# Attention in two blocks: a round's value products and scores stand together behind its transposes

## The chip, the cores and the metric

The kernel runs on one core of a Trainium2 chip. The metric is the device time of one execution in microseconds (us). The engines are TensorE (PE, matmuls and transposes), VectorE (DVE), ScalarE (ACT), GpSimd (POOL) and SyncE (SP, which issues most DMAs).

## The reference

Two transformer blocks on 512 tokens of width 1024, in float32. The two places that matter here are their attentions. The first block has a local attention (8 heads) and a dilated attention (12 heads in 3 groups). The second block has two layers; its first is an attention with 16 query heads over 512 latent and 256 context tokens:

```
def neighbourhood_attention(q, k, v, rpb):
    ...
    scores = jnp.einsum('brqhd,brkhd->bhrqk', qg, kn).astype(f32) * (dh ** -0.5) + bias[None]
    scores = jnp.where(mask, scores, NEG_INF)
    p = jax.nn.softmax(scores, axis=-1).astype(v.dtype)
    o = jnp.einsum('bhrqk,brkhd->brqhd', p, vn)

def gqa_attend(q, k, v):
    s = jnp.einsum('bkgqd,bksd->bkgqs', q, k, preferred_element_type=jnp.float32) * (HEAD_DIM_2 ** -0.5)
    p = jax.nn.softmax(s, axis=-1).astype(v.dtype)
    return jnp.einsum('bkgqs,bksd->bkgqd', p, v)

def dilated_window_attention(q, k, v, window, dilation):
    ...
    p = jnp.exp(scores - lse[..., None]).astype(v.dtype)
    o = jnp.einsum('nhbqk,nbkhd->nbqhd', p, vb).reshape(-1, lp, h, dh)[:, :seg]
```

The dilated attention runs once for each group, and the groups' outputs are weighted by their softmax denominators. Around the attentions stand dense projections, gated feed-forward layers and, at the end, a gated recurrent layer (the HGRN mixer), which the change doesn't touch.

## The kernel before

The program is made in two steps. A planner (`build_program`) writes a list of steps, each with the semaphores that it waits for. Then every engine gets its own instructions of each step, in the order of that list. So one list sets the order on all queues: if a step stands ahead of another in the list, its parts stand ahead on PE, on DVE and on ACT.

Dense products are exact to float32 by a split: an operand is a rounded part and a rest (`SHI` and `SLO` of a weight, `hh` and `hl` of an activation, `HLh` and `HLl` of the input), and a product is three matmuls (lines 2517 to 2519), with 512 or 256 columns. ACT rounds a weight tile (line 2084) and POOL makes the rest (line 2254).

Attention works on pairs of heads (two items, h = 0 and 1). A pair passes through four steps:

- `s1`, a `Score` step: PE multiplies queries and keys (line 2537, from partitions 0 to 63 for one head and 64 to 127 for the other), into two areas of PSUM (`scores`, banks 0 to 3). DVE takes the maximum (line 2368; in the first block with the mask added, line 2365), ACT takes the exponential into `e` and its sum into `m` (line 2119).
- `s2`, one to three `Flip` steps: PE transposes `e` (line 2544), four blocks of 128 columns at a time into one bank (three in the dilated attention), and ACT and DVE in turn copy the bank into `pt` (lines 2125 and 2373).
- `shares`, two `Share` steps: DVE takes the reciprocal of the sum (line 2377), ACT makes the diagonal matrix `dg` from it (line 2129).
- `s3`, a `Pv` step, and `normed`, an `OutNorm` step: PE multiplies `dg` by ones (line 2550) and the values by `pt` (line 2554), both with 64 output partitions a head; ACT and DVE normalise into `o` (lines 2133 and 2381), and that frees the bank. `finish` then writes an `OutSplit` step: ACT rounds `o` into `hh` (line 2137), POOL makes the rest.

Round i of the loop in `attention` has the transposes of pair i - 2, the value products of pair i - 3 and the scores of pair i. There are 72 rounds with scores: 16 of the local attention (256 or 384 keys), 8 of the dilated one (768 keys) and 48 of the second block's. There, six pairs belong to one query tile, with 768, 256, 768, 768, 256 and 768 keys.

`attention` is a generator. At each `yield` the function `weave` may place dense work: it keeps a count of work for both sequences and goes on with the one that is behind. In the second block the dense sequence is, for each query tile, the projection of the next one with its head norm and rotary step (`qk2`: a square on ACT at line 2107, a matmul at line 2525, a logarithm and an exponential on ACT at lines 2111 and 2113, a multiplication on DVE at line 2352, a matmul at line 2529) and the output projection of the one before (`out2`, whose sums DVE adds at line 2395).

Transposes, value products, head norms and dense sums share four PSUM banks (4 to 7). `take` hands them out in the order in which `give` put them back, so a change of order in the plan also changes which step waits for which bank. The first PE instruction that writes a bank waits for whoever read it last.

Of the kernel before, what the change touches and what calls it, by code (L numbers as in the profile page):

```python
# [241 lines left out]
def build_program(nc, t_in, out):  # L242
# [3 lines left out]
    def put(step):  # L246

        plan.append(type(step)(*map(frozen, step)))

    def tick(name, n=1):  # L250

        count[name] = count.get(name, 0) + n
        last[name[0]] = (name, count[name])
        return (name, count[name])

    def all_now():
        return [last[e] for e in "pavg" if e in last]
# [13 lines left out]
    def place(name, shape, dt, at):  # L271
        return nc.alloc_sbuf_tensor_at(name, shape, dt, offset=at)

    def fixed(name, n, dt=F32, size=4):
        at = base[0]
        base[0] += (n * size + 31) // 32 * 32
        return place(name, [128, n], dt, at), at

    XL, _ = fixed("XL", 8 * NT)
    XC, XC_at = fixed("XC", 8 * NC)  # L280
    HLh, _ = fixed("HLh", 8 * NT, F32R)
    HLl, _ = fixed("HLl", 8 * NT, F32R)
# [6 lines left out]
    CONST, _ = fixed("CONST", 640)  # L289
    COL, _ = fixed("COL", NCOLS)  # L290
    MOD1, _ = fixed("MOD1", 48)
    MOD2, _ = fixed("MOD2", 96)
    MOD3, _ = fixed("MOD3", 96)
    COEF, _ = fixed("COEF", 48)
    SMALL, _ = fixed("SMALL", 16)
    ROPE, _ = fixed("ROPE", 1024)
    LBS, _ = fixed("LBS", 40)
# [10 lines left out]
    def take():  # L308
        return banks[free_banks.pop(0)]

    def give(b, *tok):
        b.free = list(flat(tok))
        free_banks.append(banks.index(b))
# [91 lines left out]
    def arena(specs, free, end=END):  # L405
        at, rings = AR, {}
        for name, (n, cols, dt, size) in specs.items():
            aps = []
            for i in range(n):
                aps.append(place(f"{name}_{names[0]}", [128, cols], dt, at)[:, :])  # L410
                names[0] += 1
                at += (cols * size + 31) // 32 * 32
            rings[name] = Ring(aps, free)
        assert at <= end, at - end
        return rings

    names = [0]
    emitted = set()

    def after(key):  # L420
        while key not in emitted:
            yield "wait"
# [61 lines left out]
    def slots(cells):  # L484
        for i, c in enumerate(cells):
            c.raw, c.at = f"d_ada{names[0]}", 0
            names[0] += 1
        return cells
# [240 lines left out]
    def attention(items, W, finish):  # L729
        st, exps, dgs = {}, {}, {}  # L730

        def s1(pair):
            mms, t_q, used = [], [], []
            for it in pair:
                mm, t = it["scores"]()
                work[0] += 2 * sum(at.stop - at.start for at, _, _ in mm)
                mms.append(mm)
                t_q += t
                used.append((it["e"](), W["m"].next(), scores.next()))
            n = pair[0]["n"]  # L740
            masks, t_mask = zip(*(it.get("mask", (None, None)) for it in pair))
            t_mm, t_max, t_exp = tick("p_score", 2), tick("v_max", 2), tick("a_exp", 2)
            put(Score(mms, [ps.ap[:, 0:n] for _, _, ps in used], [e.ap[:, 0:n] for e, _, _ in used],
                      [m.ap for _, m, _ in used], masks, t_q, [ps.free for _, _, ps in used], t_mm,
                      [e.free for e, _, _ in used], [m.free for _, m, _ in used], t_mask, t_max, t_exp))
            for h, (it, (e, m, ps)) in enumerate(zip(pair, used)):
                one = lambda t: (t[0], t[1] - 1 + h)
                ps.free = [one(t_max) if masks[h] else one(t_exp)]
                if "masked" in it:
                    it["masked"](one(t_max))  # L750
                st[id(it)] = (e, one(t_exp))
                exps[id(it)] = (m, one(t_exp))
                it["scored_by"](t_mm)
# [31 lines left out]
        def shares(it):  # L785

            m, t_exp = exps.pop(id(it))
            d = W["dg"].next()
            t_rec, t = tick("v_rec"), tick("a_share")
            put(Share(m.ap, d.ap, t_exp, t_rec, d.free, t))  # L790
            m.free = [t]
            d.rdy = [t]
            dgs[id(it)] = d

        def s3(pair):

            ps, at, toks = zip(*(st.pop(id(it)) for it in pair))
            ds = [dgs.pop(id(it)) for it in pair]
            nk = pair[0]["n"] // 128  # L800
            b = take()
            vals = [[it["values"](j) for j in range(nk)] for it in pair]
            work[0] += 512 * nk + 512
            t_mm = tick("p_pv")
            put(Pv([p.ap[:, 128 * a:128 * (a + nk)] for p, a in zip(ps, at)], nk, b.ap, [[v for v, _ in vs] for vs in vals], [d.ap for d in ds], list(toks),
                   vals[0][0][1], [d.rdy for d in ds], b.free, t_mm))
            for c in (*ps, *ds):
                c.free = [t_mm]
            return b, t_mm

        def normed(b, t_mm):
            o = W["o"].next()
            t_rb, t = tick("a_rb"), tick("v_onorm")
            put(OutNorm(b.ap, o.ap, t_mm, o.free, t_rb, t))
            give(b, t)
            return o, t

        pairs = [items[i:i + 2] for i in range(0, len(items), 2)]
        n = len(pairs)
        for i in range(n + 4):  # L820
            turn, read = 0 <= i - 2 < n, 0 <= i - 3 < n
            turns = s2(pairs[i - 2]) if turn else iter(())
            for _ in turns:
                yield
                break
            if read:
                done = normed(*s3(pairs[i - 3]))
                yield
            yield from turns
            if turn:  # L830
                for it in pairs[i - 2]:
                    shares(it)
            if read:
                finish(pairs[i - 3][0], *done)
                if "done" in pairs[i - 3][1]:
                    emitted.add(pairs[i - 3][1]["done"])
            if i < n:
                for key in pairs[i][0].get("needs", ()):
                    yield from after(key)
                s1(pairs[i])  # L840
                if "scored" in pairs[i][1]:
                    emitted.add(pairs[i][1]["scored"])
                yield

    def out_split(o, t_o, src, hi, lo, t_free):
        t1, t2 = tick("a_ohi"), tick("g_olo")
# [144 lines left out]
    def marked(items, needs, name):  # L991
# [31 lines left out]
    W = arena({"va": (1, 4 * 512, F32, 4), "qa": (4, 512, F32, 4), "vb": (1, 3 * 4 * 256, F32, 4),  # L1023
               "qb": (6, 512, F32, 4), "mk": (1, 1536, F32, 4), "bi": (5, 384, F32, 4), "e": (4, 384, F32, 4),
               "f": (4, 512, F32, 4), "pt": (3, 768, F32, 4), "r": (2, 512, F32, 4), "o": (2, 128, F32, 4), "dg": (2, 128, F32, 4),
               "m": (8, 8, F32, 4)}, [])
# [11 lines left out]
    early = slots([Cell(place(f"early{i}", [128, USZ], F32, AR + 4 * USZ * i)[:, :]) for i in range(12)])  # L1038
# [422 lines left out]
    W = arena({"hh": (6, 512, F32R, 4), "hl": (6, 512, F32R, 4), "f": (4, 512, F32, 4), "r": (2, 512, F32, 4)}, blk, c_at)  # L1461
# [43 lines left out]
    for c in W["r"].cells:  # L1505
# [14 lines left out]
    W = arena({"f": (4, 512, F32, 4), "r": (2, 512, F32, 4), "hh": (2, TT, F32R, 4), "hl": (2, TT, F32R, 4),  # L1520
               "q": (2, TT, F32, 4), "k": (2, TT, F32, 4), "v": (1, 6 * 256, F32, 4), "e": (4, TT, F32, 4),
               "pt": (2, 2 * TT, F32, 4), "o": (2, 128, F32, 4), "dg": (2, 128, F32, 4), "m": (8, 8, F32, 4)}, blk, c_at)
# [128 lines left out]
    W = arena({"hh": (6, TT, F32R, 4), "hl": (6, TT, F32R, 4), "f": (4, TT, F32, 4), "r": (2, 512, F32, 4)}, all_now(), c_at)  # L1651
    hid = hids(W)

    def with_mask(main):
        for i, _ in enumerate(main):
            if i == 20:
# [12 lines left out]
    W = arena({"v": (1, 6 * 256, F32, 4), "xy": (4, 2 * TT, F32, 4), "kk": (2, TT, F32, 4), "q": (2, NT, F32, 4),  # L1669
               "sg": (2, NT, F32, 4), "t": (2, TT + 1, F32, 4), "ek": (1, TT + 1, F32, 4), "eq": (1, NT, F32, 4),  # L1670
               "R": (1, 2 * NT, F32, 4), "A": (1, NT, F32, 4), "kt": (1, TT + 1, F32, 4), "S": (4, 128, F32, 4),
               "f": (1, NT, F32, 4), "r": (1, NT, F32, 4), "hh": (2, NT, F32R, 4), "hl": (2, NT, F32R, 4),
               "pe": (4, 8, F32, 4), "de": (4, 8, F32, 4)}, blk)
# [347 lines left out]
    W = arena({"hh": (6, NT, F32R, 4), "hl": (6, NT, F32R, 4), "f": (4, NT, F32, 4), "r": (2, 512, F32, 4)}, all_now())  # L2021
# [678 lines left out]
```

## Time and profile before

| What | Value |
|---|---|
| median of 3 runs | 2769.22 us (2765.15 to 2774.45) |
| span of the profiled execution | 2768.6 us |
| PE busy | 2622.1 us, 95% of the span |
| DVE, ACT, POOL busy | 56%, 40%, 36% |
| mean granted TensorE clock | 0.983 |

The profiled execution's span lies 0.6 us under the median of the runs, so the two can be set against each other without a correction. A granted clock of 1.00 is 2.4 GHz, of 0.50 it is 1.2 GHz. Busy shares of PE are high everywhere because matmuls overlap each other; what a stage loses is seen in the gaps between its instructions.

### The profile page before, as it was taken

What the parts mean: (1) busy time and instruction counts of PE and PEld (TensorE: products, weight loads), DVE (VectorE), ACT (ScalarE), POOL (GpSimd) and SP (SyncE); (2) the same over time, 40 slices, a digit from 0 to 9 for tenths busy, and PEclk for the clock granted to TensorE, in tenths of its full rate; (3) what the DMA queues carried; (4) which work ended last, traced back from release to release, by engine and by line L of the source; (5) the groups of instructions that cost most, each with busy time, mean ns of one, the idle gap of its engine ahead of it and who ended that gap; (6) DMA issues with size and microseconds to landing.
All of it is one profiled execution on the core that took longest, in us unless ns stands there. A gap on an engine that the chain in (4) does not pass through costs nothing. (4 is left out here: it accounts for less than half of the span.)

```text
span 2768.6 us, 39433 instructions
## 1 busy us (share of the span) xinstructions
PE 2622.1 (95%) x15278; PEld 2194.3 (79%) x15278; DVE 1545.5 (56%) x2406; ACT 1108.5 (40%) x2041; POOL 988.8 (36%) x571
## 2 busy tenths in 40 slices
PE   7997989899999999997999999998899997899998
PEld 5765778888888867776988888898788886788887
DVE  5454256654565355656765555656768677622324
ACT  4553442422323455555312112235555556522222
POOL 4344634445545312223323323342212212444444
PEclk9998999999999999999999999999999999999999
DMA  8633224343333100001333333311111110122222
GB/s 303 222 138 130 73 96 159 122 145 130 130 136 116 39 16 24 24 32 44 115 126 118 123 114 122 129 69 62 39 46 62 54 54 32 61 99 95 95 99 76
DMA packets 81465, 267.83 MB, mean 97 GB/s; under 512 B 8704, under 2 KB 16512, under 8 KB 81280
## 3 DMA queue, kind: packets, MB, share of 16 engines
q1 hardware_dynamic: 78944, 259.68, 26.8%
q10 hardware_dynamic: 2048, 4.33, 0.4%
q8 instruction: 122, 2.00, 0.3%
q0 software_dynamic: 288, 1.31, 0.1%
q14 instruction: 63, 0.52, 0.1%
HBM read 260.57 MB, written 4.72 MB: 96 GB/s over the span
## 5 line engine op out<-in xcount | busy, mean ns | idle before, releaser
L2254 POOL TENSOR_TENSOR SLO<-RAW,SHI 128x1024 fp32r<-128x1024 f32 (+1 forms) x290 | 704.9, 2433 | 1078.4 <-ACT SHI L2084 1073.0
L2084 ACT ACTIVATE SHI<-RAW 128x1024 fp32r<-128x1024 f32 (+1 forms) x334 | 344.9, 1037 | 969.6 <-PE PS L2519 967.9
L2517 PE MATMUL PS<-HLh,SHI 128*128 128x512 f32 (+1 forms) x1800 | 704.3, 391 | 11.5 <-POOL SLO L2254 5.6
L2519 PE MATMUL PS<-HLh,SLO 128*128 128x512 f32 (+1 forms) x1800 | 680.8, 378 | 0.0
L2518 PE MATMUL PS<-HLl,SHI 128*128 128x512 f32 (+1 forms) x1800 | 680.8, 378 | 0.0
L2517 PEld LDWEIGHTS PS<-HLh,SHI 128*128 128x128 f32 x1800 | 342.5, 190 | 82.6 <-issue 15.5
L2519 PEld LDWEIGHTS PS<-HLh,SLO 128*128 128x128 f32 x1800 | 341.8, 190 | 63.8
L2518 PEld LDWEIGHTS PS<-HLl,SHI 128*128 128x128 f32 x1800 | 342.7, 190 | 60.7 <-issue 5.8
L2517 PE MATMUL PS<-hh,SHI 128*128 128x512 f32 (+1 forms) x1024 | 366.2, 358 | 8.2 <-POOL SLO L2254 3.9
L2519 PE MATMUL PS<-hh,SLO 128*128 128x512 f32 (+1 forms) x1024 | 357.2, 349 | 0.0
L2518 PE MATMUL PS<-hl,SHI 128*128 128x512 f32 (+1 forms) x1024 | 355.3, 347 | 0.0
L2395 DVE SCALAR_TENSOR_TENSOR XL<-PS,MOD,XL 128x512 f32<-128x512 f32 (+1 forms) x320 | 209.8, 667 | 194.8 <-PE PS L2519 194.1
L2402 DVE TENSOR_TENSOR hl<-f,hh 128x512 fp32r<-128x512 f32 x88 | 163.9, 1863 | 121.6 <-ACT hh L2153 121.6
L2517 PEld LDWEIGHTS PS<-hh,SHI 128*128 128x128 f32 x1024 | 192.9, 188 | 43.0 <-issue 10.2
L2400 DVE TENSOR_TENSOR f<-f,PS 128x512 f32<-128x512 f32 x88 | 54.3, 617 | 306.8 <-PE PS L2519 285.0
L2518 PEld LDWEIGHTS PS<-hl,SHI 128*128 128x128 f32 x1024 | 193.0, 189 | 27.4 <-issue 1.2
L2519 PEld LDWEIGHTS PS<-hh,SLO 128*128 128x128 f32 x1024 | 192.8, 188 | 26.7
L2517 PE MATMUL PS<-HCh,SHI 128*128 128x256 f32 x560 | 165.1, 295 | 11.3 <-DVE XL L2395 7.8
L2333 DVE CUSTOM_DVE_ANT_0 ADA<-cb,ADA,COL 128x1024 f32<-128x1024 f32 x96 | 175.2, 1825 | 0.0
L2519 PE MATMUL PS<-HCh,SLO 128*128 128x256 f32 x560 | 160.2, 286 | 0.0
L2518 PE MATMUL PS<-HCl,SHI 128*128 128x256 f32 x560 | 160.2, 286 | 0.0
L2333 DVE CUSTOM_DVE_ANT_0 cdump<-cb,ADA,COL 128x1024 f32<-128x1024 f32 x96 | 141.3, 1472 | 13.9 <-DMA ADA<-in_k_w 13.9
(261 smaller groups left out, 3944.9 us busy)
## 6 DMA issues: line engine op xcount, KB each, us to landing
RAW<-in_k_w SPq DMA_DIRECT2D x318, 512.0 KB, 3.5
ADA<-in_k_w SPq DMA_DIRECT2D x132, 512.0 KB, 4.3
early<-in_k_w SPq DMA_DIRECT2D x12, 512.0 KB, 15.1
RAW<-in_k_w SPq DMA_DIRECT2D x16, 256.0 KB, 2.6
XL<-in_xT SPq DMA_DIRECT2D x4, 512.0 KB, 8.1
bi<-in_k_bias SPq DMA_DIRECT2D x16, 128.0 KB, 4.4
out<-XL SPq DMA_DIRECT2D x16, 128.0 KB, 1.8
bi<-in_k_bias SPq DMA_DIRECT2D x8, 192.0 KB, 4.2
```

Of the source, the lines that this page charges most:

```text
L2084: eng.activation(u.hi, u.w, ACT.Copy).then_inc(S["a_hi"], 1)
L2254: eng.tensor_tensor(u.lo, u.w, u.hi.bitcast(F32), ALU.subtract).then_inc(S["g_lo"], 1)
L2333: eng.tensor_tensor_reduce(w if j == n - 1 else st.dump, c, w, 1.0, st.bias, ALU.mult, ALU.add, st.mod[:, j:j + 1]).then_inc(S["v_ada"], 1)
L2395: eng.scalar_tensor_tensor(out=st.x, in0=st.src, scalar=st.gate, in1=st.x, op0=ALU.mult, op1=ALU.add).then_inc(S["v_res"], 1)
L2400: eng.tensor_tensor(st.f, st.f, st.src, ALU.mult).then_inc(S["v_up"], 1)
L2402: eng.tensor_tensor(st.lo, st.f, st.hi.bitcast(F32), ALU.subtract).then_inc(S["v_ulo"], 1)
L2517: eng.matmul(st.out, lh, rh, start=st.first and j == 0, stop=False)
L2518: eng.matmul(st.out, lh, rl, start=False, stop=False)
L2519: i = eng.matmul(st.out, ll, rh, start=False, stop=st.last and j == n - 1)
```

## The change

The loop of `attention` is written anew. A round first writes all its transposes (with a chance for dense work behind each group of them), then the value products of pair i - 3, and at once behind them the scores of pair i; only then `shares` and `finish`, and one `yield`. Before, the value products stood behind the first group of transposes, with dense work after them, and the scores were the last step of the round, behind `shares` and `finish`.

Two cases (`early`) keep the value products behind the first group of transposes: where the ring `pt` is too narrow for both heads of a pair (`held`; the dilated attention), and where the queries or keys that the scores need aren't in the plan yet (`needs`).

```
@@ -820,13 +820,24 @@
         for i in range(n + 4):
             turn, read = 0 <= i - 2 < n, 0 <= i - 3 < n
             turns = s2(pairs[i - 2]) if turn else iter(())
-            for _ in turns:
-                yield
-                break
-            if read:
+            needs = pairs[i][0].get("needs", ()) if i < n else ()
+            held = W["pt"].peek().ap.shape[1] < 2 * pairs[min(i, n + 1) - 2][0]["n"]
+            early = read and (held or any(key not in emitted for key in needs))
+            if early:
+                for _ in turns:
+                    yield
+                    break
                 done = normed(*s3(pairs[i - 3]))
                 yield
             yield from turns
+            for key in needs:
+                yield from after(key)
+            if read and not early:
+                done = normed(*s3(pairs[i - 3]))
+            if i < n:
+                s1(pairs[i])
+                if "scored" in pairs[i][1]:
+                    emitted.add(pairs[i][1]["scored"])
             if turn:
                 for it in pairs[i - 2]:
                     shares(it)
@@ -834,13 +845,7 @@
                 finish(pairs[i - 3][0], *done)
                 if "done" in pairs[i - 3][1]:
                     emitted.add(pairs[i - 3][1]["done"])
-            if i < n:
-                for key in pairs[i][0].get("needs", ()):
-                    yield from after(key)
-                s1(pairs[i])
-                if "scored" in pairs[i][1]:
-                    emitted.add(pairs[i][1]["scored"])
-                yield
+            yield
```

No engine gets an instruction more or less; lines below the diff have numbers higher by 5. Three places show the new order.

**Place 1.** PE's queue in the middle of the second block's attention, around the scores (L2537) of one pair with 768 keys. L2550 and L2554 are value products, L2525 is the head norm's matmul, L2529 the rotary one, L2517 to L2519 are dense. This stands there before:

```order
L2550 MATMUL PS<-dg_192,CONST 64x128 [waits s_v_flip,s_a_share]
L2550 MATMUL PS<-dg_193,CONST 64x128
L2554 MATMUL PS<-pt_188,v_183 64x128 x12
L2525 MATMUL PS<-f_169,CONST 128x256 [waits s_a_hln,s_a_hsq]
L2537 MATMUL PS<-k_181,q_179 128x512 [waits s_a_exp]
L2537 MATMUL PS<-k_181,q_179 128x512
L2537 MATMUL PS<-k_181,q_179 128x256 x2
L2529 MATMUL PS<-f_170,CONST 128x512 [waits s_v_head]
L2517 MATMUL PS<-hh_176,SHI_60 128x512 [waits s_a_ohi,s_g_olo,s_v_onorm,s_g_lo]
L2518 MATMUL PS<-hl_178,SHI_60 128x512
L2519 MATMUL PS<-hh_176,SLO_63 128x512
L2517 MATMUL PS<-hh_176,SHI_60 128x256 [waits s_a_hln]
```

And this stands there now:

```order
L2555 MATMUL PS<-dg_192,CONST 64x128 [waits s_v_flip,s_a_share]
L2555 MATMUL PS<-dg_193,CONST 64x128
L2559 MATMUL PS<-pt_188,v_183 64x128 x12
L2542 MATMUL PS<-k_181,q_179 128x512 [waits s_a_exp]
L2542 MATMUL PS<-k_181,q_179 128x512
L2542 MATMUL PS<-k_181,q_179 128x256 x2
L2530 MATMUL PS<-f_169,CONST 128x256 [waits s_a_hln,s_a_hsq]
L2534 MATMUL PS<-f_170,CONST 128x512 [waits s_v_head]
L2522 MATMUL PS<-hh_176,SHI_60 128x512 [waits s_a_ohi,s_g_olo,s_v_onorm,s_g_lo]
L2523 MATMUL PS<-hl_178,SHI_60 128x512
L2524 MATMUL PS<-hh_176,SLO_63 128x512
L2522 MATMUL PS<-hh_176,SHI_60 128x256 [waits s_a_hln]
```

The scores follow the value products directly, and the head norm of the 256 context columns, whose bank the last row waits for (`s_a_hln`), moved behind the scores.

**Place 2.** ACT's queue at the same point. The two rows that write `e` are the exponentials of those scores. Before:

```order
L2111 ACTIVATE r_174<-PS,SMALL 128x512
L2113 ACTIVATE r_174<-r_174 128x512
L2133 ACTIVATE o_190<-PS 128x128
L2111 ACTIVATE r_173<-PS,SMALL 128x256
L2113 ACTIVATE r_173<-r_173 128x256
L2129 ACTIVATE dg_192<-CONST,m_196 128x128
L2129 ACTIVATE dg_193<-CONST,m_197 128x128
L2137 ACTIVATE hh_175<-o_190 128x128
L2119 ACTIVATE e_186,m_200<-PS,m_200 128x768
L2119 ACTIVATE e_187,m_201<-PS,m_201 128x768
L2125 ACTIVATE pt_188<-PS 128x512
```

Now:

```order
L2116 ACTIVATE r_174<-PS,SMALL 128x512
L2118 ACTIVATE r_174<-r_174 128x512
L2138 ACTIVATE o_190<-PS 128x128
L2124 ACTIVATE e_186,m_200<-PS,m_200 128x768
L2124 ACTIVATE e_187,m_201<-PS,m_201 128x768
L2134 ACTIVATE dg_192<-CONST,m_196 128x128
L2134 ACTIVATE dg_193<-CONST,m_197 128x128
L2142 ACTIVATE hh_175<-o_190 128x128
L2116 ACTIVATE r_173<-PS,SMALL 128x256
L2118 ACTIVATE r_173<-r_173 128x256
L2130 ACTIVATE pt_188<-PS 128x512 x2
```

Both exponentials moved ahead of `dg`, of the rounding of `o`, and of the logarithm and exponential of the head norm (`r_173`).

**Place 3.** PE's queue near the end of this attention, where no dense work is left: from the transposes of one round to its scores. Before:

```order
L2544 MATMUL PS<-CONST,e_184 128x128 [waits s_v_flip]
L2544 MATMUL PS<-CONST,e_184 128x128 x3
L2550 MATMUL PS<-dg_192,CONST 64x128 [waits s_v_onorm,s_a_share]
L2550 MATMUL PS<-dg_193,CONST 64x128
L2554 MATMUL PS<-pt_189,v_183 64x128 [waits s_a_flip,s_v_flip]
L2554 MATMUL PS<-pt_189,v_183 64x128 x11
L2544 MATMUL PS<-CONST,e_184 128x128 x2
L2544 MATMUL PS<-CONST,e_185 128x128 x6
L2537 MATMUL PS<-k_182,q_180 128x512 [waits s_a_exp]
```

Now:

```order
L2549 MATMUL PS<-CONST,e_184 128x128 [waits s_v_flip]
L2549 MATMUL PS<-CONST,e_184 128x128 x3
L2549 MATMUL PS<-CONST,e_184 128x128 [waits s_a_flip]
L2549 MATMUL PS<-CONST,e_184 128x128
L2549 MATMUL PS<-CONST,e_185 128x128 x2
L2549 MATMUL PS<-CONST,e_185 128x128 [waits s_v_flip]
L2549 MATMUL PS<-CONST,e_185 128x128 x3
L2555 MATMUL PS<-dg_192,CONST 64x128 [waits s_v_onorm,s_a_share]
L2555 MATMUL PS<-dg_193,CONST 64x128
L2559 MATMUL PS<-pt_189,v_183 64x128 x12
L2542 MATMUL PS<-k_182,q_180 128x512 [waits s_a_exp]
```

The value products moved from behind the first four transposes to behind all twelve, and nothing stands between them and the scores.

## Rows read from the trace of the kernel before

**Rows 1.** The head of the page.
```profile
span 2768.6 us, 39433 instructions
```

**Rows 2.** Busy time by stretch (PE first): the second attention, one tile's six rounds.
```profile
950.00:1290.00 340.00, 318.19 (x2519) 236.61 (x2517) 191.62 (x414) 193.13 (x501) 77.63 (x85) 0.99 0.08 26
1093.90:1138.10 44.20, 43.22 (x336) 32.42 (x335) 26.30 (x56) 24.93 (x64) 10.16 (x11) 1.00 0.08 25
```

**Rows 3.** PE's timeline, second block: start us, duration us, count, [idle before].
```profile
1092.35 1.56 PE L2537 MATMUL PS<-k,q 64*128 64x512 f32 x8
1093.84 0.39 PE L2517 MATMUL PS<-HCh,SHI 128*128 128x256 f32 x1
1094.06 0.28 PE L2518 MATMUL PS<-HCl,SHI 128*128 128x256 f32 x1
1094.18 0.28 PE L2519 MATMUL PS<-HCh,SLO 128*128 128x256 f32 x1
...
1094.66 0.60 PE L2544 MATMUL PS<-CONST,e 128*128 128x128 f32 x4
1095.09 1.02 PE L2525 MATMUL PS<-f,CONST 128*128 128x512 f32 x2
1096.50 0.44 PE L2550 MATMUL PS<-dg,CONST 128*64 128x128 f32 x4 [0.39 <-DVE pt L2373]
...
1098.75 0.67 PE L2525 MATMUL PS<-f,CONST 128*128 128x256 f32 x2 [0.49 <-ACT r L2111]
1099.35 1.56 PE L2537 MATMUL PS<-k,q 64*128 64x512 f32 x8
```

**Rows 4.** ACT's timeline in the same stretch, and behind scores of 256 keys.
```profile
1092.82 0.30 ACT L2137 ACTIVATE hh<-o 128x128 fp32r<-128x128 f32 x1
...
1096.61 0.20 ACT L2119 ACTIVATION_READ_ACCUMULATOR e<-PS,m 128x1 f32 x1
1096.70 1.05 ACT L2084 ACTIVATE SHI<-RAW 128x1024 fp32r<-128x1024 f32 x1
...
1097.91 0.69 ACT L2111 ACTIVATE r<-PS,SMALL 128x512 f32<-128x512 f32 x1
1098.63 0.63 ACT L2113 ACTIVATE r<-r 128x512 f32<-128x512 f32 x1
...
1099.45 0.47 ACT L2111 ACTIVATE r<-PS,SMALL 128x256 f32<-128x256 f32 x1
...
1101.00 0.69 ACT L2129 ACTIVATE dg<-CONST,m 128x128 f32<-128x128 f32 x2 [0.62 <-DVE m L2377]
...
1108.76 0.19 ACT L2119 ACTIVATION_READ_ACCUMULATOR e<-PS,m 128x1 f32 x1
```

**Rows 5.** DVE's timeline in the same stretch.
```profile
1099.30 0.75 DVE L2352 SCALAR_TENSOR_TENSOR f<-PS,SMALL,r 128x512 f32<-128x512 f32 x1 [2.94 <-ACT r L2113]
...
1100.41 0.48 DVE L2352 SCALAR_TENSOR_TENSOR q<-PS,SMALL,r 128x256 f32<-128x256 f32 x1 [0.16 <-ACT r L2113]
```

**Rows 6.** PE's timeline: scores of 256 keys in the second block.
```profile
1106.43 0.70 PE L2537 MATMUL PS<-k,q 64*128 64x256 f32 x4
```

**Rows 7.** PE's timeline: dilated attention.
```profile
350.02 1.57 PE L2537 MATMUL PS<-qb,qb 64*128 64x512 f32 x12
...
352.00 0.44 PE L2550 MATMUL PS<-dg,CONST 128*64 128x128 f32 x4
```

**Rows 8.** PE's timeline: the second block's attention where dense work has ended, first and last.
```profile
1253.82 1.03 PE L2537 MATMUL PS<-k,q 64*128 64x512 f32 x6
...
1286.73 1.48 PE L2554 MATMUL PS<-pt,v 128*64 128x128 f32 x24
```

**Rows 9.** The longest total wait on PE, 950 to 1290 us.
```profile
PE PS L2550 <- ACT dg L2129: 7.0, 6, 1.9
```

**Rows 10.** PE's longest single wait there; and PE's busy time, then the granted clock.
```profile
1006.05 0.70 PE L2550 MATMUL PS<-dg,CONST 128*64 128x128 f32 x4 [2.65 <-ACT r L2111]
...
1006.00:1009.40 3.40, 3.35 (x29) 0.50 0.22 63
```

## The prediction

> **What bounds the kernel now.** I read the head of the page first: the span is 2768.6 us [rows 1], 0.6 us under the median of the runs, 2769.22, so I add to the median. Then the busy time by stretch. The change touches two stretches, the attentions of the first block and that of the second. In the 340.00 us of the second PE is busy 318.19 us, DVE and ACT less than 195 each [rows 2]. In the middle of the second, one query tile's six rounds take 44.20 us with 43.22 of PE [rows 2]. So PE sets the time, its work doesn't change, and the change can only win or lose what PE waits.
>
> The timeline of such a stretch shows how little it waits: 0.39 us before the value products (for a copy of transposes) and 0.49 us before the head norm of the context columns (for ACT's logarithm) [rows 3]; the same two come back in each query tile. The list of waits names `dg` as what PE waited for longest in the second block, 7.0 us in 6 waits [rows 9].
>
> **Gain: fewer changes of the array's shape.** Scores use half the rows of the array, value products half the columns, all else the whole. The first dense matmul behind scores of 256 columns is followed by the next after 0.22 us (1093.84 to 1094.06), the later ones after 0.12 us (1094.06 to 1094.18) [rows 3], so a way back costs about 0.1 us. I take the same for a way in, which no row here shows clean. I counted neighbours in PE's whole order: pairs of different shape go from 284 to 236, and value products directly ahead of scores from 4 to 50. Two excursions become one with a change inside it. If that inner change costs 0.1 us, the sum is 48 x 0.1 = 4.8 us; if it costs nothing, 98 x 0.1 = 9.8 us less (284 to 186). I take 4.8.
>
 The exit of 0.1 us agrees; no row here shows the inner change.
>
> **Loss 1: `dg` behind the exponentials.** `shares` now stands behind `s1`, so on ACT the `dg` of pair i - 2 waits for the exponentials of pair i (place 2), and the next round's value products need it. With 768 keys the scores end at 1093.91, the last exponential at 1096.81, 2.90 us later; two `dg` take 0.69 [rows 3, 4]. So the value products can't start until 3.65 us behind the scores' end. With 256 keys it is 1107.13 to 1108.95 and the same 0.69, about 2.55 us [rows 4, 6]. Where more PE work than that stands between, it costs nothing. Where not:
>
> - No dense work left, end of the second attention. Before, it takes from 1254.85 to 1288.21, 33.4 us [rows 8]. Value products take 1.7 us with 768 keys (0.27 for `dg`, 1.48 after it) and I put 0.8 with 256; scores 1.56 and 0.70 [rows 3, 6, 8]. Now the round is a chain: 3.65 + 0.8 + 0.7, then 2.55 + 1.7 + 1.6, 3.65 + 1.7 + 1.6, 3.65 + 0.8 + 0.7, 2.55 + 1.7 + 1.6, 3.65 + 1.7, and at the end about 4.5 for twelve transposes and two more value products: 38.6 us. +5 us.
> - The same at its start, three or four rounds: +3 us.
> - The dilated attention. `held` is true, so its value products stay behind the first transposes, but `shares` moved all the same. In its last rounds scores end at 351.59 and value products start at 352.00, 0.41 us later [rows 7]; now not before 3.7 us. Six of eight rounds start them earlier than that (0.97, 0.52, 1.85, 1.85, 0.41, 0.41 us), 16 us short together. Some waits for copies inside these rounds fall away, about 4 us. +12 us.
> - One round in each query tile has two context chunks and four transposes between scores and value products, 2.65 us of work: 1 us short, five times. +5 us.
>
> **Loss 2: banks released late.** This is the largest term. In each of six query tiles the head norm of 256 columns moved behind the scores (place 1), and its logarithm on ACT behind their exponentials and `dg` (place 2). The second dense chunk behind it takes the bank that this logarithm frees. Walked from the end of the scores before, t = 0:
>
> - PE: 18 dense matmuls of 256 columns 2.1 us, four transposes 0.43, head norm 0.86 [rows 3], so 3.45; value products wait for `dg` until 3.65, end 5.35; scores until 6.95.
> - ACT: exponentials 2.90, `dg` 3.6, `hh` 3.9, weight rounding and square 5.1, logarithm 5.8, exponential 6.4 [rows 4]. DVE multiplies until 7.1, normalises until 7.3 [rows 5], and only then takes the maxima. So the last exponential of the new scores ends at 7.3 + 2.85 = 10.15, `dg` 10.85, `hh` 11.1, the logarithm of the 256 columns (0.47 [rows 4]) 11.55.
> - PE is through head norm, rotary matmul and first chunk at 9.2 and waits for that bank until 11.55: 2.35 us. The next transposes wait 0.55 for a bank that DVE's multiplication frees (exponential 0.42, then 0.48 [rows 5]), and 0.15 and 0.25 for two more.
>
> With the 0.2 above that is 3.5 us; it replaces the 0.39 and 0.49 of before [rows 3], so 2.6 net, six times: +16 us. After scores of 256 keys twelve transposes stand together and the dense chunk behind them needs the bank of the first four. Its copy is on ACT behind exponentials, `dg`, `hh` and a square: 3.9 us behind the scores, where PE is there after 2.8. 1.1 us, five times: +5 us.
>
> **Local attention.** Mostly 3.3 us of work stand between scores and value products, enough for its shorter exponentials. Two head norms come earlier than their square. I put +3 us, between 0 and 6.
>
> **Sum.** -4.8 + 5 + 3 + 12 + 5 + 16 + 5 + 3 = +44 us. 2769 + 44 = 2813 us. What hid these latencies before is the half round of transposes, value products and dense work between the `dg` and its use; that cover is what moved.
>
> **The rivals.**
>
> *A. Faster.* If PE isn't held by `dg` and banks, because waits of a few tenths sit in slack that my walks don't see, the shape changes decide: -4.8, and the 0.88 us in each of six tiles goes too, -5.3: 2759 us. Against it: where no dense work is left there is nothing to overlap with. It decides if value products there start less than 1 us behind the scores. 7%.
>
> *B. Only `dg` is late.* The bank waits of loss 2 vanish because PE, held at one place, isn't held again at the next: -4.8 - 5.3 + 25 + 3 = +18, 2787 us. For it: I walked one tile, from an even start. 20%.
>
> *C. As forecast.* 2813 us. 50%.
>
> *D. The clock falls too.* In the one place of the second attention where PE waited 2.65 us, until 1006.05, the granted clock was 0.50 for the 3.40 us from 1006.00, 1.2 GHz instead of 2.4 [rows 10]. Such a stretch does 1.7 us of work less. If six tiles and three or four rounds elsewhere each bring one, +16 us: 2829 us. Against it: most waits I find are shorter or split. The Trainium skill has the rule that idle time of PE brings the half clock back (TensorE: Matmul & The Clock Gate, part 1); the one place agrees. 18%.
>
> *E. Nothing.* Gains and losses meet within 0.3% (8.3 us, about what a measurement of this kernel can tell from no change): 5%.
>
> **Range.** C's own bounds are the local attention (6), the start (3), the dilated discount (4) and the inner change of shape (5): 2800 to 2826. With B and most of D: 2783 to 2834. A gives 7% faster, E 5% same, the rest slower.
>
> **What would show it.** In the profile after: value products about 3.65 us behind scores of 768 keys in the last rounds and in the dilated attention, with `dg` on ACT as releaser; six waits of a dense matmul of 2 us or more for ACT's logarithm (line 2116) in the second attention; a query tile of about 48 us instead of 44.20; stretches of clock 0.50 there if D holds. I am wrong if the tile stays near 44 us or below, which would mean that ACT or DVE run ahead of my walk, or if the loss lies outside both attentions.

## The result, and the profile after

The changed kernel takes 2812.13 us (median of 4 runs, 2807.48 to 2814.27), 2769.29 us before (2765.15 to 2774.45): ratio 1.0149, interval 1.0135 to 1.0163. It is slower by 1.5%. The forecast was 2813. The head of the page after; its own time beside that of before [rows 1] is 42.3 us longer:

```profile
span 2810.9 us, 39433 instructions
```

Busy time and clock of the second attention, and of one query tile from the end of its scores to the end of the next tile's (the columns are those of [rows 2]):

```profile
950.00:1331.00 381.00, 338.17 (x2594) 255.52 (x2592) 194.91 (x421) 195.34 (x511) 80.68 (x86) 0.97 0.07 23
1072.67:1120.99 48.32, 45.01 (x336) 33.76 (x335) 26.20 (x58) 24.44 (x64) 10.15 (x12) 0.96 0.07 23
```

A tile took 44.20 us with 43.22 of PE [rows 2]. It takes 4.1 us more, and PE is busy 1.8 us longer with the same 336 matmuls, at a mean clock of 0.96 instead of 1.00. The waits of PE in 950 to 1400 us:

```profile
PE PS L2555 <- ACT dg L2134: 21.1, 16, 2.9
PE PS L2522 <- ACT r L2116: 12.0, 6, 2.0
...
PE PS L2549 <- DVE XL L2400: 2.3, 6, 0.4
PE PS L2522 <- ACT pt L2130: 2.2, 5, 0.6
PE PS L2549 <- DVE q L2357: 2.1, 6, 0.4
```

Waiting for `dg` was 7.0 us in 6 waits [rows 9], now it is 21.1 in 16. The second row is new: six waits of a dense matmul for ACT's logarithm, one in each tile. Here is one of them in PE's timeline, at place 1:

```profile
1119.43 1.56 PE L2542 MATMUL PS<-k,q 64*128 64x512 f32 x8
1120.92 0.70 PE L2530 MATMUL PS<-f,CONST 128*128 128x256 f32 x2
1121.46 1.02 PE L2534 MATMUL PS<-f,CONST 128*128 128x512 f32 x2
1121.92 0.79 PE L2522 MATMUL PS<-hh,SHI 128*128 128x512 f32 x1
...
1125.18 0.39 PE L2522 MATMUL PS<-hh,SHI 128*128 128x256 f32 x1 [2.00 <-ACT r L2116]
...
1126.15 2.56 PE L2549 MATMUL PS<-CONST,e 128*128 128x128 f32 x12 [0.35 <-DVE q L2357]
```

and ACT's at the same time:

```profile
1122.11 0.90 ACT L2124 ACTIVATE e<-PS,m 128x768 f32<-128x768 f32 x1 [1.72 <-DVE m L2373]
...
1123.01 0.89 ACT L2124 ACTIVATE e<-PS,m 128x768 f32<-128x768 f32 x1
...
1123.88 0.68 ACT L2134 ACTIVATE dg<-CONST,m 128x128 f32<-128x128 f32 x2
1124.46 0.30 ACT L2142 ACTIVATE hh<-o 128x128 fp32r<-128x128 f32 x1
1124.66 0.46 ACT L2116 ACTIVATE r<-PS,SMALL 128x256 f32<-128x256 f32 x1
```

PE finished the head norm whose logarithm this is at 1121.6, and its logarithm ran at 1124.66, behind two exponentials, two `dg` and a rounding. Before, it ran at 1099.45 beside the start of the scores [rows 3, 4]. What follows the wait is the second loss:

```profile
1126.70:1130.10 3.40, 3.40 (x14) 3.06 (x14) 1.80 (x4) 1.19 (x2) 1.28 (x1) 0.50 0.00 0
```

PE had waited 2.00 and then 0.35 us, and the granted clock is 0.50, 1.2 GHz, for the 3.40 us from 1126.70. Twelve transposes took 2.56 us there and 1.48 us at full clock (1132.99, same timeline). Seven such stretches stand in the second attention now, the first at 983.3 and then one in each tile; there was one before [rows 10].

Near the end, where no dense work is left, and in the dilated attention:

```profile
1317.87 1.56 PE L2542 MATMUL PS<-k,q 64*128 64x512 f32 x8
1319.37 0.66 PE L2549 MATMUL PS<-CONST,e 128*128 128x128 f32 x4
1322.96 0.44 PE L2555 MATMUL PS<-dg,CONST 128*64 128x128 f32 x4 [2.94 <-ACT dg L2134]
...
351.82 1.57 PE L2542 MATMUL PS<-qb,qb 64*128 64x512 f32 x12
353.32 0.55 PE L2549 MATMUL PS<-CONST,e 128*128 128x128 f32 x3
357.01 0.44 PE L2555 MATMUL PS<-dg,CONST 128*64 128x128 f32 x4 [3.14 <-ACT dg L2134]
```

Scores of 768 keys end at 1319.43 and the value products start 3.53 us later, waiting for `dg`; in the dilated attention it is 3.62 us (scores end at 353.39, value products start at 357.01), where it was 0.41 [rows 7].

The difference by stage, from PE's timeline of both kernels. Most limits are the ends of rounds of scores; the local attention and the second one begin where their first scores begin, and both the dilated attention and the last stage of the second end where the last product with `dg` begins. The last column puts the forecast's terms into the same stages, its shape changes taken off; five of the six tiles lie in "five tiles":

| Stage | before, us | after, us | difference | forecast |
|---|---|---|---|---|
| local attention | 115.9 | 112.8 | -3.1 | +2 |
| from there to the dilated one's first scores | 60.8 | 60.3 | -0.5 | 0 |
| dilated attention | 113.2 | 129.0 | +15.8 | +12 |
| between the two blocks' attentions | 593.6 | 593.4 | -0.3 | 0 |
| second attention, first ten rounds | 55.5 | 55.8 | +0.3 | +2.5 |
| five tiles | 221.1 | 240.9 | +19.9 | +21 |
| last three rounds with dense work | 21.4 | 26.4 | +5.0 | +2.5 |
| without dense work | 31.6 | 36.9 | +5.3 | +5 |
| all behind it | 1482.1 | 1482.2 | +0.1 | 0 |

Over the whole span PE is busy 2630.4 us, where it was 2622.1. So 34 of the 42 us are time in which PE waits, and 8 are the same matmuls taking longer.

### The profile page after: what moved, and what is told of

Read it like the earlier page. It is cut to its first block and busy times, and to the rows that moved or that the text cites. A ratio compares the mean times of both kernels' runs of the same rounds, so it can differ in the third digit from the quotient of the medians.

```text
span 2810.9 us, 39433 instructions
## 1 busy us (share of the span) xinstructions
PE 2630.4 (94%) x15278; PEld 2205.5 (78%) x15278; DVE 1543.5 (55%) x2406; ACT 1105.4 (39%) x2041; POOL 989.2 (35%) x571
```

## The experiments

Two things in the change can be told apart. PE's order is new (value products directly ahead of scores), and ACT's and DVE's order is new (`shares` and `finish`, with `dg` and the rounding of `o`, behind the exponentials). In all experiments the computation is whole; only the order changes. Where a query tile's time is given, it runs from the end of one tile's scores to the end of the next tile's.

**e1: the new order on PE, the old one on ACT.**

```
@@ the changed kernel @@
+            if turn:
+                for it in pairs[i - 2]:
+                    shares(it)
+            if read:
+                finish(pairs[i - 3][0], *done)
...
             if i < n:
                 s1(pairs[i])
...
-            if turn:
-                for it in pairs[i - 2]:
-                    shares(it)
-            if read:
-                finish(pairs[i - 3][0], *done)
...
```

> The changed kernel with one thing put back: shares and finish stand ahead of the scores in the plan, so dg and the rounding of o are ahead of the exponentials on ACT again, while PE keeps value products and scores back to back. My theory (dg behind the exponentials and banks released late cost the time): the dg waits go (in the dilated attention, at start and end of the second, one round a tile, some 25 us), and the bank waits get shorter by the 1.0 us of two dg and one rounding, 6 times, but stay, since the head norm still stands behind the scores: about 2777 us, 2770 to 2785. Rival, the PE order itself is what costs (value products and scores together, whatever ACT does): it stays at 2805 to 2812 us. Rival, everything is ACT's order: 2760 to 2769 us.

Measured: 2763.26 us (2758.21 to 2767.29), ratio 0.9981, interval 0.9972 to 0.9991. All of the loss is gone, and 0.2% more. My 2777 was 14 us too high, and the time is that of the rival "everything is ACT's order". But the stages, in the table below, speak against that rival too: the five tiles are still 8.7 us longer than before, while the start of the second attention is 7.3 us shorter, the local attention 4.3 and the end 3.1, gains that I had put at nothing. PE's waits, 950 to 1400 us:

```profile
PE PS L2522 <- ACT r L2116: 6.8, 6, 1.1
PE PS L2542 <- ACT e L2124: 4.9, 6, 1.5
...
PE PS L2555 <- ACT dg L2134: 2.6, 4, 1.6
```

The waits for `dg` fall from 21.1 us to 2.6. Those for the logarithm fall too, from 2.0 to 1.1 us each, though PE's order still has the head norm behind the scores: with `dg` and the rounding ahead of the exponentials, the logarithm has two `dg` and a rounding fewer ahead of it. So the late `dg` makes the bank waits longer, but isn't their only cause.

**e2: the other half alone, `shares` and `finish` late, PE's order as before.** The same two blocks, moved behind `s1` in the kernel before:

```
@@ the kernel before @@
             if i < n:
...
                 s1(pairs[i])
...
+            if turn:
+                for it in pairs[i - 2]:
+                    shares(it)
+            if read:
+                finish(pairs[i - 3][0], *done)
...
+            yield
```

> The kernel before with one thing moved: shares and finish stand behind the scores, PE's order of value products, dense work and scores stays. My theory: dg is then ready 3.6 us after scores of 768 keys and 2.3 us after scores of 256, and before there are only 0.4 to 3.3 us of PE work between; dilated +15, end of the second attention +5, and about 7 us in each query tile: 2820 to 2835 us, slower than the change itself. Rival, the PE order is what costs: within 5 us of 2769.

Measured: 2864.47 us (2860.69 to 2867.37), ratio 1.0344, interval 1.0329 to 1.0360: +94 us, twice the loss of the change itself and 30 us above the 2820 to 2835 expected. The tiles (6.7 us each for 7) and the dilated attention (16.1 for 15) came as expected; the start of the second attention (17.0) and the local one (6.9) weren't counted at all, and the end took 15.1 us and not 5. The waits, in the same stretch:

```profile
PE PS L2550 <- ACT dg L2129: 63.4, 42, 2.9
```

In 42 of the 48 rounds of the second attention the value products wait for `dg` now. Where the value products stand behind the first four transposes, as before, they come at once upon the late `dg`; behind all twelve and the dense work between them (the change), most of it is covered. So PE's new order hides more than half of what the new order on ACT costs.

**e3: the change in the local attention alone.** The kernel before, with the changed kernel's loop body taken while pairs of the local attention are in turn (`shares` late there too):

```
+            if W["pt"].cells[0].ap.shape[1] == 768 and pairs[min(i, n + 1) - 2][0]["n"] < 768:
...
+                continue
```

> The new order in the local attention alone, the order of before in the dilated and in the second block's. In the changed kernel's trace the local attention ends 3.3 to 3.8 us earlier than before. If that is the order's own gain, this kernel takes 2765 to 2766 us; if it was chance (where a clock stretch fell), 2769.

Measured: 2774.16 us (2772.25 to 2779.19), ratio 1.0018, interval 1.0009 to 1.0028: slower than before, where both sides expected it no slower. The local attention is 3.1 us shorter, as in the whole change, and the dilated attention 5.5 us longer, though its own rounds have the old order. Its first value products are those of the last local pairs:

```profile
250.41 0.44 PE L2579 MATMUL PS<-dg,CONST 128*64 128x128 f32 x4 [2.58 <-ACT dg L2158]
...
258.24 0.70 PE L2579 MATMUL PS<-dg,CONST 128*64 128x128 f32 x4 [3.14 <-ACT dg L2158]
```

Their `dg` stood behind the exponentials of 768 keys: 2.58 and 3.14 us, and a lower clock behind the second. The price of a late `dg` is that of the scores ahead of it, not of its own pair.

**e4: the change, with one more `yield` between value products and scores**, so that dense work can stand there.

```
             if read and not early:
                 done = normed(*s3(pairs[i - 3]))
+                yield
             if i < n:
```

> The changed kernel with a place for dense work between value products and scores; all transposes still stand ahead of the value products, shares and finish still behind the scores. My theory: the head norm of 256 columns goes back ahead of the scores, so the bank waits of 2 us and more (6 times, about 16 us with what follows) go; the dg waits stay or grow a little, as less work stands between scores and the next value products: 2795 to 2812 us. Rival, back to back is itself the cost: 2770 to 2780.

Measured: 2837.89 us (2834.55 to 2840.39), ratio 1.0248, interval 1.0233 to 1.0264: slower than the change, which neither side expected. The waits show why:

```profile
PE PS L2556 <- ACT dg L2135: 36.1, 22, 2.9
...
PE PS L2523 <- ACT pt L2131: 6.8, 5, 1.4
```

Dense work is limited. What is placed between value products and scores no longer stands between scores and the next value products, where it covers the late `dg`: from the end of scores to the next value products PE is busy 4.4 us on the mean in the tiles of the change, 3.3 in those of e4 and 2.1 in those of e2. The waits for `dg` are 36.1 us instead of 21.1. One half of the theory held: the head norm is back ahead of the scores, and the waits of 2.0 us for the logarithm are gone. So the back-to-back placement isn't the harm.

**e6 and e7: which of the two late steps?** Both are the changed kernel; e6 has `shares` alone ahead of the scores, e7 `finish` alone:

```
@@ e6 @@
+            if turn:
+                for it in pairs[i - 2]:
+                    shares(it)
             if i < n:
                 s1(pairs[i])
...
@@ e7 @@
+            if read:
+                finish(pairs[i - 3][0], *done)
...
             if i < n:
                 s1(pairs[i])
```

> The changed kernel with only shares (the reciprocal and dg) ahead of the scores; finish (the rounding of o and its rest) stays behind them. Theory (the late dg is the root of nearly all of the loss, the waits for banks too, because a head norm's logarithm is late when maxima and exponentials are late): close to the first experiment, 2763 to 2772 us; the six waits of the dense chunk for the logarithm 1.0 to 1.4 us each. Rival (the bank waits are a loss of their own, by what stands on ACT between exponentials and logarithm): rounding adds 0.3 us to each of them, and dense chunks of the output projection wait for a late hh: 2775 to 2785 us.

> The changed kernel with only finish ahead of the scores; shares (the reciprocal and dg) stays behind them. Theory (the late dg is the root): about the changed kernel's time, 2805 to 2815 us, with some 20 us of waits for dg in the second attention. Rival (the late rounding of o and the banks are a third or more of the loss): 2785 to 2800 us.

Measured: e6 2768.70 us (2767.39 to 2770.84), ratio 0.9996, interval 0.9987 to 1.0005; e7 2813.23 us (2809.96 to 2815.72), ratio 1.0153, interval 1.0140 to 1.0167. Waits of e6, then of e7:

```profile
PE PS L2522 <- ACT r L2116: 7.9, 6, 1.3
...
PE PS L2555 <- ACT dg L2134: 2.9, 4, 1.6
```

```profile
PE PS L2555 <- ACT dg L2134: 21.5, 17, 2.9
PE PS L2522 <- ACT r L2116: 10.2, 6, 1.7
```

Both times are those of the theory. `shares` is the root: early, it takes away 43 us; `finish` early takes away nothing that can be measured alone, and some 5 us beside `shares` (e6 against e1). On the logarithm each acts as its length on ACT says: 2.0 us late with both behind, 1.7 without the rounding (0.30 us), 1.3 without `dg` (0.68), 1.1 without both.

**e9: the other loss alone.** The change, with `early` also true in the one round of each tile in which the context columns' head norm stands, so that the value products go back behind the first transposes and the head norm comes ahead of the scores again.

```
-            early = read and (held or any(key not in emitted for key in needs))
+            early = read and (held or any(key not in emitted for key in needs)
+                              or n == 48 and i % 6 == 3)
```

> The changed kernel as it is (shares and finish behind the scores), with the value products in their old place in one round of each query tile of the second attention: the round in which the context columns' head norm stands, which so comes ahead of its scores again, and before whose scores dg and the rounding stand on ACT as before. This takes out loss 2's mechanism alone. Theory (loss 2 as the prediction priced it, 16 us, though a part of it came as a lowered clock): the six waits on the logarithm go, the stretches of clock 0.50 in each tile go too, a tile takes 45 to 46 us instead of 48.2; 2812 - 14 = 2798 us (2793 to 2802). Rival (the engine queues are late anyway, since dg is late, and PE waits at the next place instead): waits for dg in the second attention grow from 21 us to 28 or more, and the time stays above 2805 us.

One clause of that isn't so: `dg` and the rounding stay behind the exponentials in this round too. Measured: 2798.53 us (2794.61 to 2800.19), ratio 1.0103, interval 1.0081 to 1.0126: 13.6 us less than the change, where the theory said 14. The waits, and a tile:

```profile
PE PS L2556 <- ACT dg L2135: 20.5, 15, 2.9
```

```profile
1114.83:1159.67 44.84, 43.32 (x335) 32.52 (x335) 26.35 (x56) 24.35 (x64) 10.17 (x11) 1.00 0.07 25
```

The waits on the logarithm are under 0.3 us each, those for `dg` haven't grown (the rival is out), PE is busy 43.32 us again, and the clock is 1.00. The five tiles lose 1.8 us instead of 19.9. The edit moves the value products of that round as well, but in the tiles of the change PE didn't wait ahead of those; it waited for the logarithm. So the loss in the tiles is the head norm's place, waits and clock together.

**e8 and e5: what is left of e1's losses.** e8 is e1 with the same edit as e9. e5 is e1 with `n == 48 and 9 <= i < 42` in that place.

> The changed kernel with shares and finish ahead of the scores, and with the value products in their old place in one round of each query tile of the second attention only: the round in which the context columns' head norm stands (place 1), which so comes ahead of the scores again. Theory (the 1.7 us a tile of the first experiment come from this head norm's late logarithm, 1.1 us a wait on the context chunk's bank): the six waits on the logarithm fall under 0.6 us, a tile takes 44.2 to 44.6 us instead of 45.9, five tiles -6 to -8 us against the first experiment: 2755 to 2758 us. Rival (the tile's loss lies in all its rounds, with copies and dg): a tile stays at 45 us or more, 2760 to 2765 us.

> The changed kernel with shares and finish ahead of the scores (as in the first experiment), but from the tenth to the forty-second round of the second attention with scores the value products stand where they stood before (early is true). So local attention and both ends of the second attention have the new place of the value products, the middle has the old one. Theory (the new place gains where ACT's order is left alone, and in the middle it costs 1.7 us a tile because the context columns' head norm stands behind the scores there): the first experiment's stages add up, -4.3 + 1.8 in the local attention, -7.3 at the start of the second, -3.1 and -1.3 at its end, 0 in the dilated attention and 0 in five tiles: 2770 - 14 = 2756 us (2753 to 2760). Rival (the first experiment's gains at the start are borrowed from the tiles: what PE doesn't wait at the start it waits later): the tiles lose again about what the start gained, 2762 to 2766 us.

Measured: e8 2753.25 us (2748.81 to 2756.53), ratio 0.9938, interval 0.9926 to 0.9951; e5 2756.82 us (2755.06 to 2760.52), ratio 0.9951, interval 0.9937 to 0.9964. Both are faster than either kernel. A tile of e8:

```profile
1082.10:1125.82 43.72, 43.13 (x336) 32.50 (x335) 26.23 (x58) 25.27 (x64) 10.15 (x11) 1.00 0.08 25
```

43.72 us, 0.5 under the 44.20 of before; the five together are 3.7 us shorter, more than expected, which puts e8's time 2 us below its range. e5 came as its theory had it: its middle is as before (0.0) and its gain at the start (-5.4) stays, so that gain is no loan from the tiles. Of e1's -7.3 there, 1.9 are only moved: in e1 the stage has 362 matmuls, in e5 and before it has 366, and the four come later. The 5.4 us are again a wait and its clock: PE's wait of 2.65 us until 1006.05 and the stretch of 0.50 behind it [rows 10] aren't there in e5. In that stage its waits come to 4.5 us where they were 7.8, and PE is busy 45.55 us where it was 47.68, at a clock of 1.00 where it was 0.97.

All of them by stage, as difference to the kernel before in the profiled executions (what stands ahead of the local attention, 0 to -2.8 us, and what stands behind the second one, -1.3 to +3.4 us, isn't shown; both and the stretch between the attentions have no edit in them and show how far two executions differ: 5.4 of the 21.6 us by which e8's is shorter lie there):

| Stage | after | e1 | e2 | e3 | e4 | e5 | e6 | e7 | e8 | e9 |
|---|---|---|---|---|---|---|---|---|---|---|
| local | -3.1 | -4.3 | +6.9 | -3.1 | +5.7 | -4.4 | -4.3 | -3.3 | -4.4 | -3.1 |
| to the dilated one's first scores | -0.5 | +1.8 | -0.1 | +0.8 | +2.4 | +2.0 | -0.4 | -0.6 | +0.9 | +0.3 |
| dilated | +15.8 | 0.0 | +16.1 | +5.5 | +14.4 | +0.1 | -0.7 | +16.1 | -0.9 | +15.5 |
| between | -0.3 | +0.2 | 0.0 | +0.7 | -0.8 | +0.1 | -0.8 | -0.4 | -4.3 | -0.9 |
| first ten rounds | +0.3 | -7.3 | +17.0 | 0.0 | +9.0 | -5.4 | -7.1 | +0.1 | -5.4 | +3.1 |
| five tiles | +19.9 | +8.7 | +33.7 | -0.1 | +21.3 | 0.0 | +9.5 | +16.2 | -3.7 | +1.8 |
| last three with dense | +5.0 | +2.7 | +3.4 | 0.0 | +2.1 | 0.0 | +4.3 | +5.0 | +0.3 | +0.8 |
| without dense | +5.3 | -3.1 | +15.1 | 0.0 | +7.6 | -3.1 | -2.7 | +9.9 | -3.0 | +7.8 |

## Why the prediction was right

**Direction, size and main places: right.** 2813 was forecast and 2812.13 measured, and the stages with the largest terms came out near theirs: tiles, dilated attention, end. e1 shows that the whole loss hangs on the order on ACT and DVE, e9 that the tiles' part of it needs the head norm behind the scores as well. That two losses add up (rival B against C) is decided by e9: without the logarithm's waits 13.6 us go, and 27.5 us of loss remain.

**Loss 1, `dg` behind exponentials: right.** 3.65 us was walked for 768 keys, 3.53 and 3.62 measured. The end of the attention took +5.3 for +5 (the chain in the forecast adds up to 38.8 us and not to its 38.6; from the same start to the same end, 1291.79 to 1330.47, it took 38.7). In the dilated attention PE's waits for `dg` are 18.0 us in 8, and before it waited 2.6 for `dg` and 2.5 for copies that it now doesn't wait for: +12.9 for the 12 forecast. The other 3 us of the stage's 15.8 are longer busy time (110.39 us for 107.23), at a mean clock of 0.93 where it was 0.98:

```profile
PE PS L2555 <- ACT dg L2134: 18.0, 8, 3.1
```

```profile
246.20:375.30 129.10, 110.39 (x676) 82.82 (x674) 41.80 (x96) 56.22 (x119) 48.89 (x31) 0.93 0.16 52
```

At the start the +0.3 hides +2.2: four matmuls fewer stand in that stage (362 against 366), 1.9 us by e1 against e5. Forecast +3.

**"One round a tile waits for `dg`", 5 x 1: wrong in size.** That round waits 0.19 us in a tile of after. As I read it, though no run tests it, the walk set out from an even start, and PE, held up 2 us earlier in the tile, comes to that round with ACT ahead of it.

**Loss 2, banks released late: right in mechanism, and its size was part wait, part clock.** Walked: 2.35 us on the logarithm and 0.55, 0.15 and 0.25 for transposes. Measured: 2.00, and 0.35 and 0.39. The copy behind scores of 256 keys was put at 1.1 and is 0.39. So a tile waits 0.39 + 2.00 + 0.35 + 0.39 + 0.19 = 3.32 us where it waited 0.88, +2.4 instead of the 4.6 that the terms gave (2.6 + 1 + 1). The rest of the +4.0 a tile, 1.6 to 1.8 us of busy PE, is the clock, which I had put into rival D as something on top of C. In the sixth tile (the last three rounds with dense work) nothing had been waited for before: 2.9 us of waits and 2.1 of longer busy PE are the +5.0. **So the total was right for a partly wrong reason, and by luck:** the forecast put some 49 us on waits, 5 less for shape changes and nothing on the clock; the whole span has 34 us more of waits and 8 of longer busy time. Waits were priced 15 us too high, 11 of them in the five tiles (2.2 in each). Busy time was put 13 us too low, by the clock and by shape changes that gave less. The two errors nearly cancel.

**Rival D**, in part true: the clock falls once in each tile. Over the whole span the mean clock went from 0.983 to 0.978, so 2768.6 x 0.017 = 47 and 2810.9 x 0.022 = 62 us of work were given up, each good to 1.4 us: about 15 more, where D said 16. Not all of it cost time, since a part of each stretch fell on waits. e1 gives their price clean, since the same wait of 1.1 us stands in all its tiles and the clock fell in only two of five. A tile without and one with:

```profile
1047.54:1092.82 45.28, 43.41 (x335) 32.54 (x335) 26.19 (x56) 25.37 (x65) 10.16 (x11) 1.00 0.08 24
1092.82:1139.86 47.04, 44.98 (x335) 33.82 (x335) 26.31 (x56) 25.28 (x65) 10.15 (x11) 0.96 0.08 24
```

1.76 us, against the 1.7 of the forecast. The Trainium skill's rule that idle time of PE brings the half clock back (TensorE: Matmul & The Clock Gate, part 1) points the right way. Here a stretch of it followed waits of 2.00 and 0.35 us in six tiles out of six, and in e9's tiles, without them, in none.

**Local attention: wrong sign.** +3 was put, and the stage took -3.1. Its waits for `dg` are 0.9 us as before; 3.3 us of work was cover enough. The gain is no clean one: seven matmuls fewer stand in the stage (673 against 680). Taken to the dilated one's first scores the counts are equal (913) and -3.6 remains. The mean clock up to there went from 0.96 to 0.97, and with it PE's busy time from 157.0 to 153.7 us: nearly all of the -3.6 is busy time, by my estimate the clock and nine more merged pairs of different shape (0.9 us). How much of e1's -4.3 there is its own stays open.

**Shape changes: the inner change is as forecast, the gain from it smaller.** A change between two half shapes costs as much as one to the whole: 24 value products that start at 1135.72 and at 1142.49 in the timeline of after are followed by scores at 1137.13 and by a dense matmul at 1143.90, 1.41 us both times.

```profile
1135.72 1.48 PE L2559 MATMUL PS<-pt,v 128*64 128x128 f32 x24
1137.13 1.56 PE L2542 MATMUL PS<-k,q 64*128 64x512 f32 x8
...
1142.49 1.48 PE L2559 MATMUL PS<-pt,v 128*64 128x128 f32 x24
1143.90 0.50 PE L2522 MATMUL PS<-hh,SHI 128*128 128x512 f32 x1
```

So one of two entrances is saved and not both. The Trainium skill's "Changing tiling mode (not just tile) drains the TensorE" (TensorEngine Tiling (Array Packing), Key Properties) agrees. The 0.1 us for a saved entrance stays an estimate. In e8's five tiles, with four merged pairs each, it would give 2.0 us, and PE is busy only 0.8 us less there (214.77 for 215.54). The other 3.0 of the 3.7 us are waits, 5.1 us before and 2.1 in e8: mostly the 0.39 and 0.49 us of [rows 3], which fall away.

**Rival A** had the sign of e1 and nearly its time (2759 against 2763), but by luck. Its 5.3 us were to come from the tiles, which took 8.7 us more in e1; what made e1 faster are the two ends of the second attention and the local one, where A had only shape changes.

## What to carry to other kernels

When one list sets the order of all queues, moving a step on the bounding engine moves its parts on every other engine; check there which short instructions that somebody waits for (`dg`, a logarithm that frees a bank) now stand behind long ones, and keep those ahead. The same late instructions cost 94 us in the old order on PE (e2) and 49 us in the new one (the change against e1), where more work stood between their queueing and their use, and a `yield` that moved this work made it worse. An edit that looks bad as a whole can hold a gain: split it by engine, and here its PE half, with one round a tile exempt, made the kernel 0.6% faster.

## What the runs showed of the hardware

- The clock fell at waits shorter than I had expected: 2.00 us and 0.35 us soon after it were followed by 3.40 us at 1.2 GHz in every tile of after. The shorter the wait for the logarithm, the fewer of the six tiles had such a stretch: 6 at 2.0 us (the change), 5 at 1.7 us (e7), 3 at 1.3 us (e6), 2 at 1.1 us (e1), none where it was under 0.3 us (e9); each is one execution. So a wait of 1.1 us is priced between 0 and 1.8 us beyond itself. Two executions of one kernel may differ by it, which no run here shows.
- Value products directly ahead of scores, half the columns and then half the rows, cost the same entrance as value products ahead of a full-array matmul (1.41 us from first to next, above).
